# Attention bias from 128 spread copies of its rows, one output job on split operands, filler matmuls and a finer first load

## The reference: what is computed

```
proj = rms_norm(x) @ w_in          # q, k, v, iq, ik, iw, glu_in
score = einsum(relu(iq . ik), iw); sel = top 64 keys of each query
logits = q . k[sel] * 128**-0.5 + rel_bias[rel_bucket(t - sel)]
attn = softmax(logits) @ v[sel]
conv = silu(layer_norm(depthwise_conv(a * sigmoid(g), width 31)))
x = x + concat([attn, conv]) @ w_out
```

## Time and profile before

| | us |
|---|---|
| median of three executions | 1590.39 (1587.97 to 1590.80) |
| the profiled execution, its own time | 1592.55 |
| its span | 1590.7 |
| TensorE busy in it | 1535.6 (97%) |
| VectorE busy | 1388.4 (87%) |
| ScalarE busy | 1079.6 (68%) |
| mean granted TensorE clock | 0.985 of full |

### The profile page before, as it was taken

The page is one execution under the profiler, slowest core; times in us unless marked ns, Lnnn a source line. Parts: engine busy times, 40 slices in busy tenths (PEclk is TensorE's granted clock), DMA queues, the critical chain, the costliest instruction groups (busy, mean ns, idle before and its releaser), DMA issues.

```text
span 1590.7 us, 21547 instructions
## 1 busy us (share of the span) xinstructions
PE 1535.6 (97%) x7366; PEld 1258.5 (79%) x7366; DVE 1388.4 (87%) x1693; ACT 1079.6 (68%) x1284; POOL 10.7 (1%) x23
## 2 busy tenths in 40 slices
PE   7999999998999999999999997899999999999998
PEld 6998895576788878888887886678887888888886
DVE  4788989654999999999999986699999999999997
ACT  5444352163878877877877785587877887787785
POOL 0000100000000000000000000000000000000000
PEclk9999999998999999999999998999999999999999
DMA  8954442353799999989999992199999999999993
GB/s 239 334 186 142 152 157 80 132 175 141 264 388 370 363 359 378 369 333 374 385 355 356 381 360 92 62 335 380 375 366 360 372 366 340 377 369 366 354 374 146
DMA packets 159004, 469.51 MB, mean 295 GB/s; under 512 B 20811, under 2 KB 40733, under 8 KB 158661
## 3 DMA queue, kind: packets, MB, share of 16 engines
q1 hardware_dynamic: 157540, 466.85, 79.9%
q10 hardware_dynamic: 1376, 1.54, 0.3%
HBM read 466.24 MB, written 2.11 MB: 294 GB/s over the span
## 4 chain that ended last, share of the span: by engine, by line
PE 88%; DVE 8%; ACT 1%; issue 1%; DMA 1%; DVEq 0%; SPq 0%; POOL 0%
PE ps L1754 26%; PE ps L1756 25%; PE ps L1755 25%; PE ps L1836 3%; DVE split_lo L1077 3%; PE ps L1711 2%; PE ps L2077 2%; PE ps L2063 1%; PE ps L1740 1%; DVE work L1122 1%; DVE cat L1077 1%; DMA ring<-in_w_in_e 1%; PE ps L1865 0%; ACT split_hi L675 0%; DVE work L1243 0%
## 5 line engine op out<-in xcount | busy, mean ns | idle before, releaser
L675 ACT ACTIVATE split_hi<-ring 128x1024 fp32r<-128x1024 f32 x856 | 900.6, 1059 | 303.0 <-PE ps L1756 277.0
L1077 DVE TENSOR_TENSOR split_lo<-ring,split_hi 128x1024 fp32r<-128x1024 f32 x856 | 1021.8, 1219 | 93.6 <-ACT split_hi L675 58.8
L1754 PE MATMUL ps<-split_hi,cat 128*128 128x512 f32 (+1 forms) x1728 | 682.2, 395 | 11.0 <-DVE split_lo L1077 5.4
L1756 PE MATMUL ps<-split_hi,cat 128*128 128x512 f32 (+1 forms) x1728 | 671.8, 389 | 0.0
L1755 PE MATMUL ps<-split_lo,cat 128*128 128x512 f32 (+1 forms) x1728 | 671.7, 389 | 0.0
L1754 PEld LDWEIGHTS ps<-split_hi,cat 128*128 128x128 f32 x1728 | 325.6, 188 | 93.0 <-issue 16.1
L1756 PEld LDWEIGHTS ps<-split_hi,cat 128*128 128x128 f32 x1728 | 325.0, 188 | 67.7
L1755 PEld LDWEIGHTS ps<-split_lo,cat 128*128 128x128 f32 x1728 | 325.6, 188 | 63.8 <-issue 0.5
L1754 PE MATMUL ps<-cat,split_hi 128*128 128x256 f32 x384 | 111.8, 291 | 8.5 <-DVE split_lo L1077 4.9
L1756 PE MATMUL ps<-cat,split_lo 128*128 128x256 f32 x384 | 110.4, 288 | 0.0
L1755 PE MATMUL ps<-cat,split_hi 128*128 128x256 f32 x384 | 110.4, 287 | 0.0
(11 more groups left out here) (198 smaller groups left out, 659.8 us busy)
## 6 DMA issues: line engine op xcount, KB each, us to landing
ring<-in_w_gate SPq DMA_DIRECT2D x128, 1024.0 KB, 6.5
ring<-in_w_up SPq DMA_DIRECT2D x128, 1024.0 KB, 6.6
ring<-in_w_down SPq DMA_DIRECT2D x128, 1024.0 KB, 6.3
ring<-in_w_in_e SPq DMA_DIRECT2D x32, 512.0 KB, 4.9
ring<-in_w_in_e SPq DMA_DIRECT2D x16, 1024.0 KB, 5.2
ring<-in_w_out_e SPq DMA_DIRECT2D x16, 1024.0 KB, 5.2
ring<-in_pool_w_o SPq DMA_DIRECT2D x4, 1024.0 KB, 7.4
x_sb<-in_x SPq DMA_DIRECT2D x4, 512.0 KB, 7.9
```

Source lines behind the costliest of these rows:

```text
L675: return nc.scalar.activation(out, in_, ACT.Copy, scale=scale)
L1077: return tt(dst, full, hi.bitcast(F32), ALU.subtract)
L1754: mm(out, sh, mh, start=start, stop=False, **how)
L1756: return mm(out, sl, mh, start=False, stop=stop, **how)
```

## The change

Four things are done. The bias rows are spread to 128 copies in DRAM by one DMA and loaded already in the right order, and the flips go. `wa3` becomes a split job, whose operand `attnT` is itself split, with the layer norm's steps placed anew around it. x is loaded by quarters, and the first weight block in two halves. Filler matmuls, which nothing reads, are put before waits of TensorE.

```diff
-    jobs = [("ag0", (0, 1)), ("ag1", (4, 5)), ("flip0", (2, 3)), ("flip1", (2, 3)), ("kvi", (6, 7)), ...
+    jobs = [("ag0", (0, 1)), ("ag1", (4, 5)), ("kvi", (6, 7)), ("iq0", (4, 5)), ("kT", (0,)),
-STREAM += [(f"wc{n}", 4) for n in range(4)]
-DIRECT = [f"wa{n}" for n in range(4)]
+STREAM += [(name, 4) for name in ("wa3", "wc0", "wc1", "wc2", "wc3")]
+DIRECT = [f"wa{n}" for n in range(3)]
...
+        attn_parts = cat_cut(2 * D, HEADS, SEQ)
+        bias_rows = nc.dram_tensor("bias_rows", [P, HEADS * 512], F32, kind="Internal").ap()
+        def first_bank(j):
+            return 2 + j % 6
...  (SyncE)
+                if b == 0:
+                    for dst, src in parts(s):
+                        sp.dma_start(dst[:, 0:2, :], src[:, 0:2, :]).then_inc(first_in, 16)
+                    load_x(1)
+                    for dst, src in parts(s):
+                        sp.dma_start(dst[:, 2:4, :], src[:, 2:4, :]).then_inc(mixer_in[s], 16)
+                    load_x(2)
+                    load_x(3)
+                    continue
...  (ScalarE)
-            act.dma_start(bias_up, bass.AP(tensor=bias_dram.tensor, offset=0,
-                                           ap=[[1, P], [512, HEADS], [1, SEQ]])).then_inc(bias_loaded, 16)
+            act.dma_start(bias_rows, bass.AP(tensor=bias_dram.tensor, offset=0,
+                                             ap=[[0, P], [1, HEADS * 512]])).then_inc(bias_spread, 16)
             split_past("ag0", 5)
             gate_tanh(0)
             split_past("ag1", 3)
             gate_tanh(1)
             split_past("ag1", 6)
-            flipped_out(0)
-            split_past("kvi", 2)
-            flipped_out(1)
+            act.wait_ge(bias_spread, 16)
+            act.wait_ge(sq_done, 8)
+            act.dma_start(bias_sb, bass.AP(tensor=bias_rows.tensor, offset=P - 1,
+                                           ap=[[HEADS * 512 - 1, P], [512, HEADS], [1, SEQ]])).then_inc(bias_loaded, 16)
...
-            split_past("ag3", 2)
+            act.wait_ge(oT_out, 4)
+            copy(attn_parts[0], attnT).then_inc(attn_hi, 1)
+            split_past("ag3", 4)
             for h in range(2):                     # squares of conv
...
-            split_past("ag3", 4)
+            split_past("wa3", 2)
...  (ScalarE, in the loop over the four pairs)
+                if j in (1, 2):
+                    split_past("wa3", 2 + j)
...  (VectorE)
-            for n in range(2):
-                convolve(31)
-                add_job(f"wa{n}")
+            convolve(31)
+            dve.wait_ge(attn_hi, 1)
+            low(attn_parts[1], attnT, attn_parts[0]).then_inc(attn_lo, 1)
+            add_job("wa0")
+            convolve(CONV_TAPS)
             split_past("ag3", 2)
-            convolve(CONV_TAPS)
             wait_job("mean")
...                                                # mean_sb, two subtractions
-            add_job("wa2")
             split_past("ag3", 4)
+            add_job("wa1")
             wait_job("var")
...                                                # rvar, rstd_diag
+            add_job("wa2")
+            split_past("wa3", 2)
             scale_conv(0)
             scale_conv(1)
             silu(0)
             scale_conv(2)
             silu(1)
             lo_of_conv(0)
             scale_conv(3)
             silu(2)
             lo_of_conv(1)
+            split_past("wa3", 3)
             silu(3)
             lo_of_conv(2)
+            split_past("wa3", 4)
             lo_of_conv(3)
             add_job("wa3")
...  (TensorE)
+            def keep_busy_small(n):
+                for i in range(n):
+                    mm(ps[:, 0, 0:P], ones[:], ones[:], start=True, stop=True)
+            pe.wait_ge(set_up, 1)
+            keep_busy_small(24)
             pe.wait_ge(ident_in, 16)
+            def keep_busy(n, bank):
+                for i in range(n):
+                    mm(ps[:, bank, 0:SEQ], ones[:], const_sb[:, 0:SEQ], start=True, stop=True)
...                                                # flip_bias and its calls are gone
             def beside_ag0(q):
-                if q == 1:
-                    for j in range(4, 8):
-                        turn_first(j)
-                pe.wait_ge(xT_out, max(2, q + 1))
+                if q in (2, 3):
+                    turn_first(2 * q)
+                    turn_first(2 * q + 1)
+                pe.wait_ge(xT_out, 8 if q == 5 else q + 1)
...                                                # mean(1) from wa3 q 0 to wa2 q 2; var from wa3 q 2 to q 0; rstd from q 3 to q 2
             for j in range(4):
                 turn_first(j)
+                if j % 2:
+                    keep_busy_small(8)
...
-            direct_job("wa3", attnT, beside_wa3)
+            pe.wait_ge(attn_lo, 1)
+            out_job("wa3", attn_parts, beside_wa3)
...
+            keep_busy(2, 6)
             pe.wait_ge(x_added, 16)
             turn_x(0, 3)
             def moe_pe(l):
+                keep_busy(1, 2 if l else 6)
                 route_x(l, 3)
                 ...
                 last.then_inc(router_done, 1)
+                keep_busy(4, 2 if l else 6)
                 pe.wait_ge(group_ready, l + 1)
                 ...                                # rank products
+                keep_busy(3, 2 if l else 6)
                 pe.wait_ge(m["pick_ready"], 1)
...
             moe_pe(0)
+            keep_busy(12, 0)
             pe.wait_ge(band_scaled, NT)
...
+            keep_busy(3, 2)
             pe.wait_ge(mix_step, 16)
             turn_x(1, 3)
```

More of the change, by code:

```diff
@@ L83, in mixer0_jobs @@
 def mixer0_jobs():
-    jobs = [("ag0", (0, 1)), ("ag1", (4, 5)), ("flip0", (2, 3)), ("flip1", (2, 3)), ("kvi", (6, 7)), ("iq0", (4, 5)), ("kT", (0,)),
+    jobs = [("ag0", (0, 1)), ("ag1", (4, 5)), ("kvi", (6, 7)), ("iq0", (4, 5)), ("kT", (0,)),
             ("iq1", (2, 3))]
@@ L308, in build @@
         rows_in = sem("rows_in")
-        x_loaded = [sem(f"x_loaded{i}") for i in range(2 * NT)]
+        x_loaded = [sem(f"x_loaded{i}") for i in range(4)]
+        first_in = sem("first_in")
         scale_in = sem("scale_in")
@@ L387, in build @@
         conv_hi = sem("conv_hi")
+        attn_hi = sem("attn_hi")
+        attn_lo = sem("attn_lo")
         conv_lo = sem("conv_lo")
@@ L522, in emptied @@
                 i = int(name[2:])
-            return {"ag": (g_scaled, i + 1), "flip": (bias_out, i + 1), "kvi": (k_scaled, 2), "iq": (iq_out, i + 1),
+            return {"ag": (g_scaled, i + 1), "kvi": (k_scaled, 2), "iq": (iq_out, i + 1),
                     "kT": (kT_out, 1), "il": (relu_done, i + 1), "q": (qn_done, 2 * i + 2), "qT": (qT_out, i + 1),
@@ L536, in _, with load_x @@
         def _(sp):
-            def load_x(half):
-                cols = slice(half * (D // 2), (half + 1) * (D // 2))
+            def load_x(quarter):
+                cols = slice(quarter * 512, (quarter + 1) * 512)
                 for t in range(NT):
-                    sp.dma_start(x_sb[:, t, cols], x_in[0, t * P:(t + 1) * P, cols]).then_inc(x_loaded[2 * t + half], 16)
+                    sp.dma_start(x_sb[:, t, cols], x_in[0, t * P:(t + 1) * P, cols]).then_inc(x_loaded[quarter], 16)
             load_x(0)
@@ L714, in _ @@
                 for k in (2 * j, 2 * j + 1):
-                    last = copy(hT[0][:, k, :], ps[:, j, (k % 2) * SEQ:(k % 2 + 1) * SEQ], gain_in_T[:, k:k + 1])
+                    last = copy(hT[0][:, k, :], ps[:, first_bank(j), (k % 2) * SEQ:(k % 2 + 1) * SEQ], gain_in_T[:, k:k + 1])
                 last.then_inc(normed_hi, 1)
@@ L718, in _ @@
             for b in range(4):
-                norm(0, [(t, b, x_loaded[2 * t + b // 2], 16) for t in range(NT)])
+                norm(0, [(t, b, x_loaded[b], 32) for t in range(NT)])
                 split_to(SPLITS + b + 1)
@@ L1103, in turned_lo @@
                 for k in (2 * j, 2 * j + 1):
-                    last = low_of(hT[1][:, k, :], ps[:, j, (k % 2) * SEQ:(k % 2 + 1) * SEQ], gain_in_T[:, k:k + 1], hT[0][:, k, :])
+                    last = low_of(hT[1][:, k, :], ps[:, first_bank(j), (k % 2) * SEQ:(k % 2 + 1) * SEQ], gain_in_T[:, k:k + 1], hT[0][:, k, :])
                 last.then_inc(xT_out, 1)
@@ L1799, in tokens_job, with kvi_job @@
                     last.then_inc(mixer_used, 1)
-            def kvi_job(between):
+            def kvi_job():
                 start_job("kvi")
                 for q in range(8):
-                    between(q)
                     w = next_unit(2, KVW + IKW)
@@ L1847, in turn_k @@
                     last = turn(ps[:, 0, SEQ + t * P:SEQ + (t + 1) * P], ik2[:, t, :])
-                last.then_inc(job_done, 1)
-            def flip_bias(i):
-                start_job(f"flip{i}")
-                pe.wait_ge(vec_out, 2)
-                pe.wait_ge(bias_loaded, 16)
-                for c in range(2):
-                    heads = slice(4 * i + 2 * c, 4 * i + 2 * c + 2)
```

(27 more changed lines are left out.)

25 lines of the change are left out of this document (8 added, 17 removed).

## The result

| | us |
|---|---|
| kernel before, six executions | 1587.12 median (1586.09 to 1590.80) |
| changed kernel, six executions | 1578.22 median (1574.97 to 1582.02) |
| ratio, 95% interval | 0.9939 [0.9924, 0.9954] |
| profiled execution, its own time and span | 1575.78, 1573.9 |
| TensorE busy, mean granted clock | 1539.9 (98%), 0.996 |

The change makes the kernel faster by 8.9 us. The forecast was 1575 with the range 1567 to 1584: direction and range held, and the point was 3.2 us too low. The gain was forecast as 15.8 us and is 8.9; why the point came closer than the gain is told further down. A second set of six gave 1576.48 (ratio 0.9935 [0.9920, 0.9951]).

What follows compares the result with a forecast made beforehand. TensorE, 88% of the chain, bounds the kernel; -2.0 - 3.4 - 3.0 - 3.8 - 2.2 - 1.4 = -15.8 us takes 1592.55 to 1576.75, less 2.16 to the median 1574.6, said as 1575; range 1567 to 1584.

Steps and rivals of the forecast that it cites:

- 1. The start: Kernel start: finer loads of x and first weight block, with small fillers holding the clock, give 2.0 us, from 0 to 3.4.
- rival (d): Fillers run at half clock from the first, a small filler's matmul taking 0.43 us: slower, 1603 us; chance 0.03.
- the cap of 3.4 us by block 4: At the start, weight block 4's late load limits the gain before the row-scale product to 3.4 us, whatever is done earlier.
- 2. The flips: Before and in `kvi`: two flips of 1.72 us leave TensorE's chain, -3.4 us, with no split late.
- rival (b): VectorE, running without a pause, takes back half the flips and the layer norm's 3 us: 1579.7 us; chance 0.15.
- my 20 us: Estimated time of the bias rows' DRAM-to-DRAM spread, issued at about 42 and needed near 68; bounds 5 and 40 us.
- rival (e): The bias spread is slow: at 40 us ScalarE stands 14 us, 1589 us in all; chance 0.03.
- 3. `wa3`: `wa3` as split job and the reordered layer norm up to `wc0`: -3.0 us, from 0 to -5.
- 4 to 6. The fillers: Fillers hold the clock at the first router (-3.8 us), pooling (-2.2) and second router (-1.4).
- Rival (a): Fillers do not keep the clock: 1589.6 us by the median, or 1583 for half of it; chance 0.11 whole or half.
- the late turn: Second router's last turn: three fillers of 1.3 us stand where TensorE waits 0.22 us, making it 1.1 us later.
- Each later place: Sign of a right forecast: places after the start, up to 240, come some 5.4 us earlier, and `wc0` some 8.4.

Runs made afterwards that it cites:

- the kernel without the first part: Changed kernel with x and block 0 loaded as before and no small fillers at the start, all else as changed: 1577.51 us, ratio 0.9928.
- The parts alone: Kernel before with one part each: bias copies 1585.55 us, `wa3` and layer norm 1585.90, fillers at routers and pooling 1581.25, finer first load without fillers 1586.23.

## Why the prediction was right, and which of its terms were not

**1. The start: -2.0 forecast, -1.0 in the profile, none in the medians.** Even the 1.0 is no more than the old start varies by itself: its five profiles have the row scale at 45.63 in the mean, the four with the changed kernel's start at 45.27. Two of the step's estimates failed. The 24 small fillers did not end at 6.3 but at 8.6, because they ran at half the pace at first. TensorE's stretches in the changed kernel (us, busy, records, clock; two records a product):

```profile
1.00:3.00 2.00, 1.92 (x9) 1.00 0.41 102
3.00:5.00 2.00, 2.00 (x11) 1.00 0.91 292
5.00:7.00 2.00, 2.00 (x20) 1.00 1.04 386
7.00:8.50 1.50, 1.50 (x15) 1.00 1.03 367
```

A product took 0.43 us before 3 and 0.2 after 5. That is the price at which rival (d) was to decide, but for ten products and not for all. With the fillers `ag0` is at 13.99 in place of 11.38, and the clock is at 2.4 GHz from 5 us up to the row scale, where the earlier trace rows had 1.2; without them it was so too from 16 us on in two of four profiles of the finer load. Second, the cap of 3.4 us by block 4 stood, but ScalarE's copies of the late turns came first, which step 1 mentioned ("so ScalarE's copies come later") and did not price: 1.87 us of TensorE.

**2. The flips: right to 0.05 us.** Every kernel with this part has 84.74 to 84.76 us in that stretch for 88.12 or 88.13 without. VectorE did not become the limit, so rival (b) fell. The spread was quicker than my 20 us. (The lower bound of 5 us was misread: 2 MB at 348 GB/s take 6.0 us.) The DMA issues of the changed kernel (KB each, median us from issue to landing):

```profile
bias_rows<-bias_dram ACTq DMA_DIRECT2D x1, 2048.0 KB, 11.2
xn<-bias_rows ACTq DMA_DIRECT2D x1, 1024.0 KB, 13.2
```

It was issued at 44.89 and had landed when ScalarE asked for it at 69.75, so rival (e) was never near. An estimate by the Trainium skill (DMA: Bandwidth & Descriptors, Latency and other measured facts) was 10 us; the trace comes close with 11.2, which is 187 GB/s of written bytes beside the weights. The crowding out of weights by long packets that the same page's rule suggested shows in no wait of that stretch.

**3. `wa3`: -3.0 forecast, -1.1 to -1.7 by itself.** The mechanism was right and the size was not. At equal clock, counted from the turns of p, the changed kernel is ahead of the kernel with the old `wa3` by 6.0 us at the squares (forecast 6.9), 2.2 at the first scaling (3.0), 2.3 at `wc0` and 1.65 at the turn behind it (3.0). Two steps of the working are mis-sized. TensorE "does not wait" at `mean`'s second half, but it waits 0.59 us there for the last taps:

```profile
289.39 1.99 PE L1933 MATMUL ps<-work,ones 128*128 128x256 f32 x8 [0.59 <-DVE work L1137]
```

And behind the start of `wc0` the splits put into the pair chain were to cost nothing; there 0.6 us are lost, 14.34 us to the turn in place of 13.70. The 1.8 us at 1.2 GHz in the working stand in the old time and in the new one and cancel. The profile's -6.2 is mostly luck: the kernel before had 10.3 us at 1.2 GHz there and the changed one 3.4. In the mean of all profiles the stretch is 92.0 us with the old form (five) and 89.7 with the new one (nine), 2.4 less; whether the new order makes the clock fall less often, the runs don't tell.

**4 to 6. The fillers: -7.4 forecast, -6.3 alone.** In the profiles the first gather's stretch gave -3.5, the pooling -2.1 and the second gather -2.4, each within 0.4 us of its term; the late turn at equal clock is the 1.1 to 1.2 us later of the forecast. Rival (a) fell with the gathers at 7.9 us. But the one profile before was dear here too. The five profiles without these fillers have 61.2, 12.4 and 20.2 us in the three stretches in the mean, those with them 58.1, 10.9 and 17.6: -3.1, -1.6 and -2.7 us. The forecast said that the half clock behind the pooling products stays. It doesn't stay the same: the kernel before had 3.1 us of it, the changed kernel's profile none, and the kernel without the first part 6 us in the same 30 us, with the same code there:

```profile
960.00:990.00 30.00, 27.50 (x114) 20.48 (x115) 19.56 (x30) 12.36 (x27) 0.00 (x0) 0.89 0.32 105
```

That execution took 34.96 us to the last turn, the changed kernel's 32.05. With the fillers the stretch is 33.3 us in the mean of seven profiles, without any 31.6 in five: 1.7 us later where 1.1 was said.

**The baseline.** This is what made the gain too large. The prices were read from an execution of 1592.55 us. In the three groups the kernel before ran 61 times with a mean of 1588.1 us and a clock of 0.988; the profiled one had 0.985. It lay 4.4 us above the typical one. The changed kernel's profile, at 0.996, lay 2.0 us below the mean of its twelve executions, 1577.8 at 0.995. So 16.8 - 4.4 - 2.0 = 10.4 us are the difference of the means, 1588.1 - 1577.8 = 10.3. The sum of 15.8 comes near the profiles' 16.8 because both hold that chance. That the point was only 3.2 us off is luck in part: the gain was 6.9 us too large, and the median of three that it was taken from, 1590.39, was 3.3 us above that of six. By the code's own terms as the two profiles give them, 1.0 + 3.4 + 1.4 + 3.5 + 2.1 + 1.3 = 12.7 us should be won, 2.4 more than the means. With the means of the profiles for the start (0.4) and for the fillers (3.1 + 1.6 + 2.7 - 1.7 = 5.7) it is 0.4 + 3.4 + 1.4 + 5.7 = 10.9. The last 0.6 us are less than one stretch at 1.2 GHz more or less makes (43.86 us without one in the fourth stretch of the table, 45.34 with), and the runs don't divide them further.

One sign came out by luck too. Each later place was to be 5.4 us earlier up to 240 and `wc0` 8.4; measured are 2.3 at the turns of p and 7.6 at `wc0` (316.85 for 324.46), because the fifth stretch gave more than its term through the clock.

The parts alone sum to 2.0 + 1.6 + 6.3 + 1.5 = 11.4 us by medians, the whole gave 8.9 and 11.2. They add up within the intervals, with no loss that needs a cause.

**What stays open.** Why the kernel with four late turns together loses part of its lead again: it had 1.4 us at the row scale and 0.6 at the turns of q. In its profile the half clock lies directly before these turns, behind a wait, and in the changed kernel it lies ahead of a wait that may take it up. First the changed kernel, then the other:

```profile
183.00:187.00 4.00, 4.00 (x24) 4.00 (x24) 4.00 (x9) 0.46 (x2) 1.56 (x3) 0.63 0.47 142
187.00:191.00 4.00, 2.62 (x22) 2.42 (x22) 3.48 (x6) 1.83 (x2) 1.81 (x2) 1.00 0.32 122
```

```profile
187.00:190.00 3.00, 1.20 (x10) 1.20 (x11) 3.00 (x7) 0.63 (x1) 0.00 (x0) 1.00 0.00 0
190.00:194.00 4.00, 4.00 (x24) 4.00 (x23) 4.00 (x8) 0.00 (x0) 0.00 (x0) 0.57 0.38 97
```

That is read from two profiles and was not tried; a filler in the wait at 187 would be the test.

## What to carry to other kernels

Before a sum is made from the profile of one execution, look where its mean clock lies among all executions, and leave out of every term what only the clock gives: compare a stretch with the same stretch at the same clock. Filler matmuls pay where TensorE's wait would have been there anyway and a block of products on the chain follows; where the wait is 0.2 us they are a cost of their own length. When a load is made finer, follow the next reader too: here TensorE's first product came about 3 us earlier without fillers, and a wait of 1.9 us for an engine in between and, in two of three profiles, a stretch at 1.2 GHz behind that wait gave most of it back.

## What was not expected of the hardware

- **The time of the same kernel varies together with its granted clock.** The kernel before ran from 1583.3 us (clock 0.990) to 1592.5 (0.986); a straight line through its runs gives about 1.4 us for each 0.001 of mean clock. With fillers the clock is 0.992 to 0.997, but the changed kernel too ran from 1574.97 (0.996) to 1582.02 (0.993).
- **Where the stretches at 1.2 GHz fall changes between kernels whose code there is the same**: in the stretch before the turn behind `wc0` they took 0, 3.4 and 6.8 us in three kernels with the old `wa3`.
- **The first matmuls of an execution ran at half pace while the rows print a clock of 1.00**: up to about 5 us in the changed kernel, and still at 18 us in the kernel without its first part.
- **A GpSimd operation on 128x4 took 0.37 us or 1.17 us**, with the same GpSimd code ahead of it.
